# Differential attention: the 16 first tokens' values by two split products over parts laid side by side, in place of one plain product

## The reference

```
s1, s2 = q1 @ k1.T * scale + bias, q2 @ k2.T * scale + bias    # per head, chunk-causal bias
a = softmax(s1) - lam * softmax(s2)
o = a @ v                                                      # v: all keys, the 16 meta tokens first
```

## Time and profile before

| | |
|---|---|
| median of 3 runs | 2591.54 us (2589.82 to 2594.27) |
| the profiled execution | 2589.82 us, of which the span is 2588.0 us |
| PE busy | 2526.3 us, 98% |
| DVE busy | 1619.0 us, 63% |
| ACT busy | 1211.9 us, 47% |
| the differential attention | about 428 to 793 us in the trace |
| in 592 to 676 us (84 us, nearly a head) | PE 81.70, DVE 75.95, ACT 61.10, POOL 19.02 us busy |

### The profile page before, as it was taken

The page is one execution under the profiler, slowest core; times in us unless marked ns, Lnnn a source line. Parts: engine busy times, 40 slices in busy tenths (PEclk is TensorE's granted clock), DMA queues, the critical chain, the costliest instruction groups (busy, mean ns, idle before and its releaser), DMA issues.

```text
span 2588.0 us, 35257 instructions
## 1 busy us (share of the span) xinstructions
PE 2526.3 (98%) x12140; PEld 2103.8 (81%) x12140; DVE 1619.0 (63%) x3515; ACT 1211.9 (47%) x2183; POOL 333.4 (13%) x368
## 2 busy tenths in 40 slices
PE   8999999999999999989999999999999999999998
PEld 7998887677667989868877888888888888888886
DVE  6123307998995777754468777867757465564765
ACT  6112314777765565554544333533335353443554
POOL 2110002222221222110000000000000001121133
PEclk9999999999999999999999999999999999999999
DMA  6324458553333111145677666666655365776787
GB/s 225 131 100 132 119 164 263 139 136 94 88 134 92 34 30 46 42 130 163 195 240 224 208 221 214 220 193 210 189 165 175 118 216 106 174 166 161 201 165 139
DMA packets 328956, 398.35 MB, mean 154 GB/s; under 512 B 20896, under 2 KB 235184, under 8 KB 320464
## 3 DMA queue, kind: packets, MB, share of 16 engines
q1 hardware_dynamic: 311216, 364.17, 44.8%
q0 software_dynamic: 17568, 31.99, 8.5%
HBM read 239.62 MB, written 156.48 MB: 153 GB/s over the span
## 4 chain that ended last, share of the span: by engine, by line
PE 62%; DVE 3%; DMA 1%; ACT 1%; issue 1%; SPq 0%; POOL 0%; DVEq 0%; ACTq 0%; POOLq 0%
PE ff_ps_x L3277 26%; PE ff_ps_m L3277 13%; PE ff_ps_z L3277 6%; PE ml_ps_s L2153 6%; PE ff_ps_m L1702 4%; PE ml_ps_o L2184 3%; PE ml_ps_t L2166 2%; DMA ml_v_raw<-scr_yT 1%; DMA ff_pieces<-scr_acc 0%; PE ff_ps_r L2714 0%; PE mo_ps_t L2731 0%; SPq L2341 0%; PE ml_ps_o L2180 0%; DVE ff_pieces L2444 0%; DMA work<-scr_w_vo 0%
## 5 line engine op out<-in xcount | busy, mean ns | idle before, releaser
L3277 PE MATMUL ff_ps_x<-ff_mv_hi_p,ff_st_hi_p 128*128 128x512 f32 x764 | 297.8, 390 | 0.5 <-ACT ff_u L3017 0.5
L3277 PE MATMUL ff_ps_x<-ff_mv_lo_p,ff_st_hi_p 128*128 128x512 f32 x764 | 297.3, 389 | 0.0
L3277 PE MATMUL ff_ps_x<-ff_mv_hi_p,ff_st_lo_p 128*128 128x512 f32 x764 | 297.2, 389 | 0.0
L2153 PE MATMUL ml_ps_s<-wide,ml_qs 128*128 128x416 f32 (+14 forms) x880 | 197.0, 358 | 3.0 <-PEq L137 2.8
L3123 DVE TENSOR_TENSOR ff_st_lo_p<-ff_ps_m,ff_st_hi_p 128x512 fp32r<-128x512 f32 x190 | 130.5, 688 | 103.4 <-ACT ff_st_hi_p L3000 103.4
L2967 POOL DMA_DIRECT2D scr_acc<-ff_pieces x64 | 55.5, 872 | 1015.3 <-DVE ff_pieces L3147 946.8
L3017 ACT ACTIVATE ff_u<-ff_ps_x 128x512 f32<-128x512 f32 x128 | 76.6, 598 | 214.9 <-PE ff_ps_x L3277 214.9
L3277 PEld LDWEIGHTS ff_ps_x<-ff_mv_hi_p,ff_st_hi_p 128*128 128x128 f32 x764 | 143.4, 188 | 32.4 <-issue 2.0
L3277 PEld LDWEIGHTS ff_ps_x<-ff_mv_hi_p,ff_st_lo_p 128*128 128x128 f32 x764 | 143.4, 188 | 29.9
L3277 PEld LDWEIGHTS ff_ps_x<-ff_mv_lo_p,ff_st_hi_p 128*128 128x128 f32 x764 | 143.4, 188 | 29.5
L2153 PEld LDWEIGHTS ml_ps_s<-wide,ml_qs 128*128 128x128 f32 x880 | 153.4, 193 | 15.3 <-issue 3.4
(11 more groups left out here) (322 smaller groups left out, 6326.1 us busy)
## 6 DMA issues: line engine op xcount, KB each, us to landing
st_raw<-in_w_ff SPq DMA_DIRECT2D x64, 512.0 KB, 6.1
scr_hid<-ff_pieces SPq DMA_DIRECT2D x128, 256.0 KB, 2.7
st_raw<-scr_hid SPq DMA_DIRECT2D x64, 512.0 KB, 5.6
ring<-in_w_ff SPq DMA_DIRECT2D x28, 1024.0 KB, 8.0
scr_t<-ring SPq DMA_DIRECT2D x24, 1024.0 KB, 6.0
ring<-scr_t SPq DMA_DIRECT2D x21, 1024.0 KB, 8.4
scr_acc<-ff_pieces POOLq DMA_DIRECT2D x64, 256.0 KB, 4.1
ring<-scr_u SPq DMA_DIRECT2D x13, 1024.0 KB, 8.0
```

What stands on the lines that cost most here:

```text
L2153: m = pe.matmul(ps_s[n % NSB][:, 0:w], q, k, start=j == 0, stop=j == len(pairs) - 1)
L3277: m = pe.matmul(bank[:, :], w[kind][:, k], a[kind][:, k], start=start and k == 0 and i == 0, stop=stop and k == KH - 1 and i == 2, skip_gr ...
```

## The change

The meta tile leaves the ring. It gets a buffer `pT_meta` (F32R) of its own, and the ring `pT` has 7 slots in place of 8 for the other tiles (`turned`, `pT_of`, `slot_free`); `put_off` goes from 7 to 6. `v_meta` is loaded twice per head, to partitions 0 to 15 and again to 32 to 47. ScalarE makes the high part of `v_meta` (128x128) just ahead of its `copy` of tile 0 of group 0, and waits for the loads there. ScalarE's copy of the meta tile rounds to F32R. A new step `split_meta`, on VectorE, stands in the list behind the turn of tile 1 of each group: for group 0 it makes the low part of `v_meta` (128x128); for every group it waits for ScalarE's copy of the meta tile and writes the low part of its first 32 partitions (32x512) to partitions 32 to 63 of `pT_meta`. The product of tile 0 is then two F32R products over 512 columns: the high values by both parts of `pT_meta`, and the low values by both. TensorE waits for `split_meta` there, and again at the turn of tile 3, which reuses the bank.

```diff
-        NPT = 8
+        NPT = 7
-        pT = mem.sb(f"da_pT", [P, NPT, 512])
+        pT = mem.sb("da_pT", [P, NPT, 512])
+        pT_meta = mem.sb("da_pT_meta", [P, 512], F32R)
+        v_meta_parts = mem.sb("da_v_meta_parts", [P, 2, P], F32R)
...
                     body_steps.append(turn)
+                    if turn[3] == 1:
+                        body_steps.append(("split_meta",) + turn[1:3])
...
-        PHASES = (((0, 1), ((1, 3),), 0.2, 7), ((2,), ((0, 0), (0, 1)), 0.15, 7), ((3,), ((0, 2),), 0.2, 7))
+        PHASES = (((0, 1), ((1, 3),), 0.2, 6), ((2,), ((0, 0), (0, 1)), 0.15, 6), ((3,), ((0, 2),), 0.2, 6))
...
-                sp.dma_start(v_meta[0:META, :], scr.v[0:META, ds(h * P, P)]).then_inc(v_loaded[0], 16)
+                for part in range(2):
+                    sp.dma_start(v_meta[32 * part:32 * part + META, :], scr.v[0:META, ds(h * P, P)]).then_inc(v_loaded[0], 16)
...
+                if (g, t) == (0, 0):
+                    act.wait_ge(v_loaded[0], 48 * (h + 1))
...
+                    act.activation(v_meta_parts[:, 0], v_meta[:, :], ACT.Copy).then_inc(v_meta_hi_ready, 1)
                 slot_free(act, h, n)
                 act.wait_ge(pT_ready, NKT * h + n + 1)
-                act.activation(pT[0:rows_of, n % NPT, c0:512], ps_t[n % NTB][0:rows_of, c0:512], ACT.Copy).then_inc(copied, 1)
+                act.activation((pT_meta if t == 0 else pT_of(n))[0:rows_of, c0:512], ps_t[n % NTB][0:rows_of, c0:512], ACT.Copy).then_inc(copied, 1)
...
+            def split_meta(h, g, **at):
+                n = kt_base[g]
+                if g == 0:
+                    dve.wait_ge(v_meta_hi_ready, h + 1)
+                    dve.tensor_tensor(v_meta_parts[:, 1], v_meta[:, :], f32(v_meta_parts[:, 0]), ALU.subtract)
+                dve.wait_ge(copied, NKT * h + n + 1)
+                to = pT_meta
+                dve.tensor_tensor(to[32:64, :], ps_t[n % NTB][0:32, :], f32(to[0:32, :]), ALU.subtract).then_inc(meta_split, 1)
...
+                if t == NTB:
+                    pe.wait_ge(meta_split, NG * h + g + 1)
...
-                pe.matmul(ps_o[:, c0:512], v_meta[:, :] if t == 0 else v[:, t - 1], pT[0:rows_of, n % NPT, c0:512],
-                          start=t == 0, stop=t == tiles_of(g) - 1).then_inc(pv_done, 1)
+                if t == 0:
+                    pe.wait_ge(meta_split, NG * h + g + 1)
+                    for part in range(2):
+                        m = pe.matmul(ps_o[:, :], v_meta_parts[:, part], pT_meta, start=part == 0, stop=False)
+                    m.then_inc(pv_done, 1)
+                    return
+                pe.matmul(ps_o[:, c0:512], v[:, t - 1], pT_of(n)[0:rows_of, c0:512],
+                          start=False, stop=t == tiles_of(g) - 1).then_inc(pv_done, 1)
```

More of the change, by code:

```diff
@@ L1232, in row, with turned, pT_of @@
             return rows[u ^ (g == 2)][:, i % 4, start:start + META + P * (i + 1)]
+        def turned(n):
+            return n - sum(base < n for base in kt_base)
+        def pT_of(n):
+            return pT[:, turned(n) % NPT]
         def comp_row(i, c, u):
@@ L1350, in slot_free @@
         def slot_free(engine, h, n):
-            if n >= NPT:
-                engine.wait_ge(pv_done, NKT * h + n - NPT + 1)
+            users = kt_base if n in kt_base else [a for a in range(NKT) if a not in kt_base and turned(a) % NPT == turned(n) % NPT]
+            if n > users[0]:
+                engine.wait_ge(pv_done, NKT * h + users[users.index(n) - 1] + 1)
             elif not (isinstance(h, int) and h == 0):
-                engine.wait_ge(pv_done, NKT * (h - 1) + last_user(n, NPT) + 1)
+                engine.wait_ge(pv_done, NKT * (h - 1) + users[-1] + 1)
         late_banks = ps_t + [ps_o]
@@ L1491, in copy @@
                 rows_of = key_cols(t)[1]
+                if (g, t) == (0, 0):
+                    act.wait_ge(v_loaded[0], 48 * (h + 1))
+                    if not (isinstance(h, int) and h == 0):
+                        act.wait_ge(pv_done, NKT * (h - 1) + kt_base[NG - 1] + 1)
+                    act.activation(v_meta_parts[:, 0], v_meta[:, :], ACT.Copy).then_inc(v_meta_hi_ready, 1)
                 slot_free(act, h, n)
                 act.wait_ge(pT_ready, NKT * h + n + 1)
-                act.activation(pT[0:rows_of, n % NPT, c0:512], ps_t[n % NTB][0:rows_of, c0:512], ACT.Copy).then_inc(copied, 1)
+                act.activation((pT_meta if t == 0 else pT_of(n))[0:rows_of, c0:512], ps_t[n % NTB][0:rows_of, c0:512], ACT.Copy).then_inc(copied, 1)
             def out(h, g, **at):
@@ L1581, in end @@
                                          op0=ALU.mult, op1=ALU.add).then_inc(probs_ready, 1)
-            heads(dve, {"chunk": chunk, "scale": invert, "end": end})
+            heads(dve, {"chunk": chunk, "scale": invert, "end": end, "split_meta": split_meta})
             dve.wait_ge(probs_ready, NT * H)
@@ L1652, in product @@
                 if t == 0:
-                    pe.wait_ge(v_loaded[0], 32 * (h + 1))
+                    pe.wait_ge(v_loaded[0], 48 * (h + 1))
                     if not (isinstance(h, int) and h == 0 and g == 0):
```

1 line of the change is left out of this document (added).

## The result

| | before | after |
|---|---|---|
| median, four runs each | 2590.68 us (2588.25 to 2594.27) | 2639.95 us (2639.58 to 2640.18) |
| span of the profiled execution | 2588.0 us | 2638.4 us |
| PE busy | 2526.3 us, 98% | 2536.5 us, 96% |
| mean granted clock | 0.995 | 0.989 |

The ratio is 1.0189, 95% interval 1.0171 to 1.0207: the change makes the kernel 49 us slower. The forecast was 2610.5 us, with 2618 as the upper end. The sign was right; 29 us of the loss were not in it.

A forecast was written before the change was run, and what follows sets the result against it. VectorE was taken to bound each head's first and last parts, TensorE the middle. Walk 0 3.2, walks 1 to 3 14.3, last walk 0.3 and clock 3.4 made 21.2 us over 2589.82: 2611.0, put at 2610.5; range 2598 to 2618.

The forecast's parts named there:

- rival D: Whole stage: TensorE sets the time throughout, splits fit VectorE's free time, 6.6 us come off, 2583.2 us; chance 0.05.
- The sum of a walk 1 to 3: Each of walks 1 to 3: 2.7 + 0.05 + 2.4 - 0.4 = 4.8 us; three of them 14.3 us.
- group 3: Walks 1 to 3: TensorE pauses 3.3 us at P3,0 for the split, middle part ends 2.7 us late.
- group 0: Last part of a head: VectorE's split 0.71 us and low part 0.3, plus 0.05 for ScalarE's high part.
- group 1, group 2: Last part of a head or its edge: one split adds 0.71 us to VectorE.
- taken back: Each walk: the 0.41 us exp wait goes, since VectorE comes later and TensorE's products are shorter.
- the clock: Behind the three new pauses at P3,0: two falls of 1.7 us, 3.4 us; bounds 0 and 10.2.
- VectorE's work: Groups 0 to 2 of each head: three splits of 0.71 us and a low part of 0.3, 2.4 us.
- Walk 0: Head 0, without group 3: value load wait 1.2 us, groups 2.4, less 0.4: 3.2 us.
- The load wait: Head 0: ScalarE waits for the value load, making VectorE's reciprocal 1.2 us late (0.4 to 1.9).

The follow-up runs named there:

- ceiling: Kernel before, its order and seven products put off, with two short F32R products of high parts for the plain product, no split: 2593.74 us.
- no_split: As order_only, but two short F32R products of high parts and ScalarE's high part of the values after their load; low parts left out, no split: 2601.24 us.
- fill: Changed kernel with throwaway identity products (8, 0, 6, 15 for groups 0 to 3) ahead of TensorE's wait at the meta product: 2627.55 us.
- work_only: As no_split, with VectorE's low part and sixteen subtractions put back, into partitions no product reads, TensorE waiting for none: 2615.97 us.
- b_both: Kernel before with the split steps in the list, executed by no engine, and a ring of 7 with six products put off: 2597.33 us.
- order_only: Changed kernel's step list, ring of 7 and separate meta tile buffer, with one plain product, no split and no wait for one: 2605.93 us.
- turn_wait: Changed kernel without the wait at the meta product, which reads high parts only; the turn of tile 3 still waits for the split: 2636.02 us.
- early: Changed kernel with the split one place earlier in the list, behind the turn of tile 0 instead of tile 1: 2612.06 us.

## Why the prediction missed

**Right: what bounds the kernel, and the sign.** A saving on TensorE counts nearly nowhere, work added to VectorE in the last part counts in full (group 0's work and the split of group 2 below), and the pause at P3,0 is 3.29 us where 3.3 was predicted. ceiling bears out the reading against rival D harder than I had put it: shorter products gain 0.00 us in a head, not 0.4. The 0.4 us per walk that I took back of the earlier trace rows, and the 0.41 given back in group 3, did not come.

The sum of a walk 1 to 3 was 4.8 us and is 12.3 to 13.0. Head 2 by terms, an estimate from the columns of the table above, as if they added (us):

| | predicted | measured |
|---|---|---|
| the order, the ring, the products put off | 0 | 1.58 (no_split) |
| group 3 | 2.7 | 2.15 (fill less no_split at chunk 33) |
| group 0, with the low part and 0.05 for ScalarE | 1.05 | 1.64 (fill, 33 to 34) |
| group 1 | 0.7 | 2.91 (fill less no_split, 42 to 48) |
| group 2 | 0.7 | 0.83 (fill less no_split, 48 to 65) |
| taken back | -0.4 | 0 |
| the clock | 1.1 | 3.83 (the changed kernel less fill) |

The group 3 term held, and half of the loss without the clock is in two terms that were too small or missing: group 1 and the order.

**Wrong, the step that failed: "TensorE stands at each of the three products for some 1.1 to 1.3 us (it comes to them up to four chunks ahead of VectorE), but it would wait for a bank anyway, and the next chunk's scores are in time"**, for group 1. In groups 0 and 2 it held but for the clock: from chunk 34 to 42, with the pause of P0,0, fill loses 0.01 us. Two things were missed. The turn of tile 3 waits for the split as well, as the section on the change says, and I priced only the wait at the product. In group 1 that turn stands right behind END 9, and TensorE arrives there 2.6 us before VectorE has done END 9 and the split, one chunk ahead of it and not four. So the next chunk's scores are not in time: from chunk 42 to 48 the changed kernel loses 3.57 us, fill at full clock 3.10, work_only 0.83. The waits in all, with the clock falls behind them, are 24 us by work_only and the changed kernel.

**Wrong in size: "the clock", two falls of 1.7 us.** I let it fall behind P3,0 alone. It fell at P0,0 too, four times of four, three of them with pauses of 1.89 us, shorter than the shortest of the earlier trace rows. fill shows 12.4 us in the median (11 by the ratios), against 3.4 predicted and 10.2 as the upper bound. Of these 2.1 are the last walk (28.2 us from END 15 to the latent attention, 26.1 in fill), where fill adds no product and the clock didn't fall either: that part is not shown to be fill's doing. The Trainium skill ("TensorE: Matmul & The Clock Gate", Part 1: The HAM clock gate) has idle or thinly used stretches bring the half clock; the trace agrees in eight of the fifteen waits for the split.

**Wrong in size: VectorE's work.** Predicted 2.4 us per head, 10 in all; 14 us in all by work_only. By the traces work_only loses 3.3 us more than no_split in head 3, and 4.5 and 4.6 in heads 2 and 1, which have a fall of the clock behind P1,0. A split costs 0.80 to 0.83 us where VectorE sets the time, not 0.71: it starts 0.11 us behind the last small record ahead of it (726.09 to 726.20), a chunk 0.04 (604.71 to 604.75). Group 3's split, which I had as free, is not quite so when TensorE doesn't pause: 0.5 to 0.8 us of it still stand at chunk 33 of work_only over no_split. In the changed kernel the pause covers it, and the group 3 term came out under the forecast. And the low part took 0.96, not 0.3: it reads two tiles of SBUF, and GpSimd's scale of row 8 had begun 0.42 us ahead of it. The Trainium skill ("SBUF — State Buffer", SBUF: two separate sides) says that a VectorE instruction with two SBUF inputs and a GpSimd one that reads SBUF exclude each other for the whole instruction. The trace agrees: the low part ends 0.14 us behind the scale, and takes 0.29 when there is none.

**Missing: the order.** Nothing in the sum stood for the moved list, the ring of 7 and the six products put off. b_both puts them at 8 us, no_split at 11 (load wait included). One piece of it is the wait at P1,0 for ScalarE's `out`, 1.1 us in each head. Another can be seen at the start of the last walk: TensorE has one product fewer to do while it waits for END 15, and its pause there is 3.64 us in no_split in place of the 2.78 of the earlier trace rows. The longer pause costs nothing by itself, since T3,0 waits for END 15 either way: from END 15 to the latent attention it is 25.7 us in the kernel before and in b_both, which has that pause at full clock. Where the clock falls in it, the stretch is longer: 27.5 us in order_only, 30.0 in no_split.

**Walk 0** was predicted at 3.2 and took 9.4 us. The load wait, 1.2 us predicted, was about 0.9; the rest is of the same kind as in the other heads: the work and the waits of groups 0 to 2, the order, and one fall of the clock (3.4 us lost).

By the runs the 49 us are: order and ring with the load wait 11, VectorE's work 14, the waits for the split 24, each to some 5 us. The clock is no fourth term but lies across all three, since TensorE also loses time to it in no_split and work_only; how much of each it makes can't be read from these runs to the microsecond. No run has the split's waits alone, so the 24 is what is left when the other two are taken off.

## What to carry to other kernels

Where an added step releases two waiting instructions, price every one of them, and where in the waiting engine's queue it stands; removing one wait (turn_wait) only hands the stall to the next, while moving the step ahead of them (early, one list position) removed more than half of the loss, VectorE's exp wait and cheaper low part included. Before pricing what a cheaper operation costs elsewhere, measure its ceiling: the cheap operation alone, in the old order, gained nothing here, which would have settled the change. And an engine that may run ahead by four buffers is not always four ahead: here it was one ahead where it had to wait, so read its lead at that place before you write "it would have waited anyway".

## What was not expected of the hardware

- VectorE's 128x128 subtraction of two SBUF tiles: 0.29 us alone, 0.95 to 0.96 beside GpSimd's scale of 1.24 us, in all four heads.
- The clock is no function of the pause just ahead of it. Behind 2.78 us it stayed at 1.00 over 7 us in the kernel before; behind 2.77 us at the same place in ceiling it was 0.52 over 7 us. At the 1.89 us of P0,0 of the changed kernel it fell three times of three, at the 2.60 us of the turn of tile 3 once in four, and behind the 1.5 us at P1,0 of work_only three times of four.
- Products of `ident` over 128 columns, whose result is thrown away (15 at P3,0, 8 at P0,0, 6 at P2,0), stood where the clock had fallen, and it was at 1.00 through the whole stage; the kernel got 12 us faster. None stood at the turn of tile 3 or in the last walk, where it didn't fall either in that run.
